# One run of modulation chunks per pair on PE, and the first head's queries in one piece

## What is computed

```python
shift, scale, gate = split(silu(c) @ w_ada + b_ada)    # for c_ctx and for c
h = rms_norm(x, norm_w) * (1 + scale) + shift
proj = h @ w_in            # 2048 -> 9 parts of 1024; each head has 128 columns of each part
...                        # two chunked recurrences per head, forwards and backwards
out = concat(o_ret, o_hgrn) @ w_out
x = x + gate * out; y = rms_norm(x, final_norm_w)
```

## Time and profile before

| | |
|---|---|
| median of 3 runs | 1432.35 us (1431.15 to 1434.57) |
| the profiled execution | 1431.82 us, its span 1430.0 us |
| PE busy | 1408.1 us, 98% of the span |
| DVE, ACT, POOL busy | 965.5, 496.3, 367.4 us |
| granted TensorE clock, mean | 0.998 |

### The profile page before, as it was taken

How to read it: one execution, slowest core, us unless ns; L and a number is a source line. 1 busy time by engine, 2 the same in 40 slices (tenths; PEclk the granted TensorE clock), 3 DMA queues, 4 the chain that set the end, 5 groups by cost and what they waited for, 6 DMA issues and landing times.

```text
span 1430.0 us, 25630 instructions
## 1 busy us (share of the span) xinstructions
PE 1408.1 (98%) x10242; PEld 1185.6 (83%) x10242; DVE 965.5 (68%) x1296; ACT 496.3 (35%) x893; POOL 367.4 (26%) x292
## 2 busy tenths in 40 slices
PE   7999999999999999999999999999999999999997
PEld 5778898889888988898889888988898888888886
DVE  4654676667888787878787878666676668632345
ACT  4332243334333433343334333423342334321234
POOL 0001114411432153215321532153115315301220
PEclk9999999999999999999999999999999999999999
DMA  9994222323332333333433333222223347183235
GB/s 378 409 418 159 78 88 88 87 84 126 126 119 96 126 126 119 98 124 126 119 104 118 126 119 110 67 86 88 94 66 97 89 147 258 46 288 109 88 104 205
DMA packets 68723, 196.64 MB, mean 138 GB/s; under 512 B 7808, under 2 KB 16272, under 8 KB 63632
## 3 DMA queue, kind: packets, MB, share of 16 engines
q1 hardware_dynamic: 68592, 195.15, 40.2%
q10 hardware_dynamic: 32, 0.02, 0.0%
HBM read 174.41 MB, written 16.53 MB: 134 GB/s over the span
## 4 chain that ended last, share of the span: by engine, by line
PE 95%; DMA 3%; DVE 1%; ACT 0%; issue 0%; SPq 0%; DVEq 0%; ACTq 0%
PE ps L1960 10%; PE ps L1962 10%; PE ps L1961 10%; PE ps L1793 8%; PE ps L1767 8%; PE ps L1794 8%; PE ps L1795 8%; PE ps L2141 5%; PE ps L2143 5%; PE ps L2142 5%; DMA area<-in_w_mod 2%; PE ps L1977 2%; PE ps L1802 2%; PE ps L1801 2%; PE ps L1800 2%; PE ps L1758 1%
## 5 line engine op out<-in xcount | busy, mean ns | idle before, releaser
L1104 DVE TENSOR_TENSOR w_lo<-area,w_hi 128x1024 fp32r<-128x1024 f32 x144 | 183.1, 1272 | 261.2 <-ACT w_hi L657 261.1
L657 ACT ACTIVATE w_hi<-area 128x1024 fp32r<-128x1024 f32 x144 | 152.5, 1059 | 481.3 <-PE ps L1962 271.6
L1960 PE MATMUL ps<-w_hi,hT_hi 128*128 128x512 f32 x640 | 252.6, 395 | 0.0
L1962 PE MATMUL ps<-w_hi,hT_lo 128*128 128x512 f32 x640 | 249.4, 390 | 0.0
L1961 PE MATMUL ps<-w_lo,hT_hi 128*128 128x512 f32 x640 | 249.3, 390 | 0.0
L1793 PE MATMUL ps<-hT_hi,w_hi 128*128 128x512 f32 x512 | 205.6, 402 | 2.1 <-DVE hT_lo L1157 2.1
L1794 PE MATMUL ps<-hT_lo,w_hi 128*128 128x512 f32 x512 | 199.8, 390 | 0.0
L1795 PE MATMUL ps<-hT_hi,w_lo 128*128 128x512 f32 x512 | 199.7, 390 | 0.0
L1960 PEld LDWEIGHTS ps<-w_hi,hT_hi 128*128 128x128 f32 x640 | 120.2, 188 | 25.9 <-issue 1.6
L1962 PEld LDWEIGHTS ps<-w_hi,hT_lo 128*128 128x128 f32 x640 | 120.1, 188 | 25.4
L1660 POOL TENSOR_TENSOR area<-area 128x320 f32<-128x320 f32 x56 | 55.7, 995 | 332.0 <-PE ps L1977 279.6
(11 more groups left out here) (263 smaller groups left out, 2460.3 us busy)
## 6 DMA issues: line engine op xcount, KB each, us to landing
area<-in_w_in SPq DMA_DIRECT2D x144, 512.0 KB, 3.6
area<-in_w_mod SPq DMA_DIRECT2D x32, 1024.0 KB, 9.6
area<-in_w_out SPq DMA_DIRECT2D x38, 512.0 KB, 3.7
gate_raw<-in_w_gate SPq DMA_DIRECT2D x32, 512.0 KB, 3.7
o_hi_scratch<-area SPq DMA_DIRECT2D x14, 320.0 KB, 2.2
o_lo_scratch<-area SPq DMA_DIRECT2D x14, 320.0 KB, 2.8
hT_hi<-o_hi_scratch SPq DMA_DIRECT2D x14, 320.0 KB, 7.1
hT_lo<-o_lo_scratch SPq DMA_DIRECT2D x14, 320.0 KB, 7.6
```

Of the source, the lines that this page charges most:

```text
L657: act.activation(w_hi[:, n % 2, :], raw[:, n % 3, :], ACT.Copy).then_inc(wt_hi.sem, 1)
L1104: v.tensor_tensor(w_lo[:, n % 2, :], raw[:, n % 3, :], w_hi[:, n % 2, :].bitcast(F32), ALU.subtract).then_inc(wt_lo.sem, 1)
L1960: mm(out, hT_hi[:, k, tile_cols(t)], w_hi[:, n % 2, w], start=k == 0, stop=False)
L1962: i = mm(out, hT_lo[:, k, tile_cols(t)], w_hi[:, n % 2, w], start=False, stop=k == KT - 1)
```

## The change

For the pairs e = 3 to 5 PE took two of the next pair's four chunks before the pair's first slice and two between its slices. Now it takes all four between the slices; pair 2 keeps its order. For e = 6 it took two before, one between the slices, then half the slices of the first queries, then the last chunk; now the four come between the slices, and the eight slices of the queries follow the pair in one piece.

```diff
             for e in range(2, WCHUNKS - 2):
                 c0 = (e + 1) * GROUP_CHUNKS
-                ada_chunk(c0)
-                if e > 2:
-                    ada_chunk(c0 + 1)
+                if e == 2:
+                    ada_chunk(c0)
                 first_group(e, 0)
-                if e == 2:
-                    ada_chunk(c0 + 1)
-                ada_chunk(c0 + 2)
-                ada_chunk(c0 + 3)
+                for c in range(c0 + 1 if e == 2 else c0, c0 + GROUP_CHUNKS):
+                    ada_chunk(c)
                 first_group(e, 1, range(0, 1))
                 modulation_columns(e + 3)
                 first_group(e, 1, range(1, 5))
             e, c0 = WCHUNKS - 2, (WCHUNKS - 1) * GROUP_CHUNKS
-            ada_chunk(c0)
-            ada_chunk(c0 + 1)
             first_group(e, 0)
-            ada_chunk(c0 + 2)
-            first_queries(0, range(0, 4))
-            ada_chunk(c0 + 3)
+            for c in range(c0, c0 + GROUP_CHUNKS):
+                ada_chunk(c)
             first_group(e, 1, range(0, 1))
             modulation_columns(e + 3)
             first_group(e, 1, range(1, 5))
-            first_queries(0, range(4, KC))
+            first_queries(0, range(KC))
             first_group(WCHUNKS - 1, 0)
```

## The result

The changed kernel is slower: 1435.73 us, median of 17 runs (1434.67 to 1437.89), against 1431.86 (1430.83 to 1434.57) for the kernel before on the same chips, +3.87 us. The ratio is 1.0027, with a 95% interval of 1.0021 to 1.0033: clear of noise, and past the 0.2% (2.9 us) that the prediction took as what can be told. The forecast was 1433.4, no measurable change, with a range of 1430.5 to 1436.0; 0.12 had gone to a slower kernel.

A forecast was written before the change was run, and what follows sets the result against it. PE and, in pairs 3 to 5, also the chunk stream were taken as full. Five saved switches and the former cover go into waiting for the stream, +1.0 us: 1432.35 + 1.0 = 1433.4 us, range 1430.5 to 1436.0.

The forecast's parts named there:

- The stream decides the rest: Pairs 3 to 6: later slot releases delay chunk loads; chunk 31 starts at 111.6 us, for +1.0 us in all.
- rival B: Pairs 3 to 6: the stream runs dry, slower by over 0.2%; +2.8 us at 6.0 us load latency; chance 0.14.
- The price L: Chunk loads: time from issue to landing of 1 MB with nothing ahead of it, taken as 5.1 us.
- the term after it: Chunk loads: landing at the later of 2.5 us after the last landing and 5.1 us after issue.
- case C: Chunk stream: no gap, later issues are hidden in the queue; -0.2 to +0.8 us; chance 0.28.
- Fewer switches: Pairs 3 to 6: joining chunk runs on PE makes five joins at 0.35 us each, saving 1.75 us.
- hT_lo: Before the first slice of pairs 3 to 6: PE waits about 0.2 us, four times, 0.8 us.
- Rival D: Pairs 3 to 6: the hT_lo wait bounds, 0.3 us each; +0.1 to +0.4 us; chance within the forecast's 0.50.
- Rival A: Pairs 3 to 6: PE-bound, the stream never late; about -1.6 us, 1430.7; chance 0.08.
- The second queries: After pair 6: PE starts them at 130.1 us against 129.13, +1.0 us that reaches the end undiminished.

The follow-up runs named there:

- the late release: Kernel before with PE's order untouched; SP holds back the loads of chunks 20, 24 and 28: 1436.68 us against 1431.31.
- pairs 3 to 5 alone: Kernel before with only pairs 3 to 5 taking their four chunks in one run, pair 6 and queries as before: 1435.58 us against 1431.18.
- pair 3 alone: Kernel before with only pair 3 taking its four chunks in one run: 1432.74 us against 1431.31.
- with 52 small matmuls: Changed kernel with 52 instead of 12 small matmuls at the very start: 1441.86 us against 1432.48 for the kernel before.
- with 92: Changed kernel with 92 instead of 12 small matmuls at the very start: 1452.63 us against 1432.48 for the kernel before.

## Why the prediction was off

*The mechanism was right and is shown.* "The stream decides the rest": a fifth slot under PE's new order removes the loss, the late release with PE's order untouched brings it, and pair by pair the waits stand before chunks 23, 27 and 31, as forecast. *The time was not.* The range held by 0.27 us, and its upper end had been set by rival B; by the prediction's own sign for B (chunk 31 after 113 us; it started at 113.96) this is case B, which had 0.14. That the range held is in part luck.

*The price L was right.* I took 5.1 us between 4.9 and 6.0; the idle-queue loads took 5.0 and 5.3, and in other runs 4.8 to 5.0 (three with a fetch near their issue took 5.5 to 6.0).

*What failed is the term after it*, "a landing at the later of (last landing + 2.5) and (issue + L)". It let the stream run at 2.5 us per MB again as soon as a gap was over. Chunk 31 was forecast to start at 111.6 and started at 113.96. Of these 2.35 us:
- 0.4 is the start: chunk 15 landed at 65.1 instead of 64.6 in this execution, so the last transposes of pair 2 came at 66.93 instead of 66.42, the run of pair 3 at 73.58 instead of 73.07, and chunk 20 landed at 79.7 instead of 79.3. The run with pairs 3 to 5 alone shows the same (transposes at 67.04).
- 1.1 is the late landing of weight chunk 5, after the first gap; chunk 23 lands behind it, at 89.5 instead of 88.1.
- 0.2 is chunk 28's L, 5.3 instead of 5.1.
- 0.7 is the late landing of chunk 29, after the second gap.

A sign that the prediction had named is missing for the same reason: the DMA share was to dip at about 88 us as well, and it doesn't, because chunk 23 landed so late that load 24 (issued at 85.9) could follow it at 2.5 us. The trace of before has one such late landing too (27 to 28: 3.5 us instead of 2.5, with a fetch that starts at 99.9 us, in a stream without a gap), and I took it for chance; I gave it a microsecond in case C and none in the sum. In that kernel it cost 0.2 us of waiting for chunk 29, and chunk 31 had three in hand. So in size the case that came is my rival B ("the stream runs dry"), 2.8 to 4.0 us, but not by its condition: L is 5.0, not 6.0. "It decides from L = 6.0 upwards" was wrong, since it weighed L alone.

*Fewer switches*: the run of four lasts from 73.58 to the next matmul at 77.29, 3.7 us, as 1.01 + 3 times 0.88 says. The switches are saved; nothing of it shows while the stream is late. With a fifth slot, and no gap, the change's order is even with the old one (1430.94 and 1430.73 us), and PE still waits for the stream at pair 6.

*hT_lo*: 3.04 us from the transposes to the next slice (66.93 to 69.97) against 3.05 forecast, 0.2 us of waiting each. Rival D is out as a bound.

*Rival A* (the stream never late) and *rival C* (no gap) fell with the first gap. The Trainium skill's estimate of 4.4 us for 1 MB (DMA: Bandwidth & Descriptors, Anatomy of one DMA), by which case C would have held, was 0.6 us short of the 5.0 measured on this path.

*The second queries* were forecast at 130.1 and came at 132.49; they are 3.36 us later than before and the span is 3.4 longer, so a microsecond there is a microsecond at the end, as forecast.

What stays open: how a fetch of 16 KB makes a landing 1.1 us late, and why only some fetches do. My reading is that the fetch occupies one of the 16 DMA engines for about a microsecond. In a stream without gaps one engine is behind anyway and the others fill up behind it, so most fetches cost nothing; a gap lets the engine catch up, and the next fetch sets it back anew. It fits the twelve gaps: in the kernel with one gap (pair 3 alone) chunk 22 is late with the fetch from 82 to 83 us, and the later fetches, from 93 and from 102 us, delay nothing (27, 28 and 29 land 2.5 us apart). It says nothing of which fetch in an unbroken stream makes one of the seven late landings there. No run took the fetches away, and the rows don't show single DMA engines; the reading is argued, not shown.

## What to carry to other kernels

Where a stream of loads and an engine are both full, look at an order of work first as an order of buffer releases: a run of uses that is cheaper for the engine releases its buffers in a burst, and the stream has only what is still on its way. The condition can be read off beforehand: the first release of the burst has to come the transfer's idle-queue latency (here 5.0 us, of which 2.5 are data) ahead of the time at which its data should land, or there is a gap. And count a gap at more than its own length: here standing still for about 1 us cost 1.4 to 2. And keep something in hand for PE: landings came up to 1.7 us late in streams without a gap too, and there the distance grew by 0.5 us at most.

A fix of one buffer more, or of one use put back ahead (one chunk of four), was enough to close the gaps and bring the time back to within what can't be told from before; to move everything back was not needed.

## What the runs showed of the hardware

- A 1 MB load into an idle queue took 4.8 to 5.3 us from issue to landing in nine readings, and 5.5 to 6.0 in three (chunk 20 with pair 3 alone and with 52 small matmuls, chunk 28 with 92), where a fetch started between 0.5 us before and 1.1 us after the issue; 2.5 us of it are its share at the stream's rate of 415 to 420 GB/s.
- After each of twelve gaps a landing next to a 16 KB instruction fetch came 0.5 to 1.6 us late, and it moved with the fetch when PE's program was shifted. In the unbroken stream of the kernel before, five of six fetches between 64 and 109 us left the landings evenly spaced to within 0.5 us, and one stood beside a landing 1.0 us late; over seven unbroken streams it was seven late landings (0.7 to 1.7 us) beside some forty fetches.
- 128-column float32 matmuls at the very start took 0.14 us a record on average (104 in 14.63 us; in the changed kernel the first 24 took 5.16), with two records for each, at a granted clock of 1.00.
